# Differential attention turned by products with diagonal scales, and rows behind down projections scaled within their last group

## The reference, cut to what matters

```
p1 = softmax(q1 @ k1.T * scale)
p2 = softmax(q2 @ k2.T * scale)
o  = (p1 - lam * p2) @ v
```

## Time and profile before

| | us |
|---|---|
| median of 3 runs | 4510.27 |
| lowest and highest run | 4505.47, 4512.88 |
| the profiled execution, its own time | 4512.04 |
| its span, first to last instruction | 4510.2 |
| TensorE busy in the span | 4217.4 |
| VectorE busy in the span | 1841.3 |
| mean granted TensorE clock, 1 being 2.4 GHz | 0.962 |

### The profile page before, as it was taken

How to read it: one execution, slowest core, us unless ns; L and a number is a source line. 1 busy time by engine, 2 the same in 40 slices (tenths; PEclk the granted TensorE clock), 3 DMA queues, 4 the chain that set the end, 5 groups by cost and what they waited for, 6 DMA issues and landing times.

```text
span 4510.2 us, 44510 instructions
## 1 busy us (share of the span) xinstructions
PE 4217.4 (94%) x17060; PEld 2839.2 (63%) x17060; DVE 1841.3 (41%) x3089; ACT 788.6 (17%) x1256; POOL 643.3 (14%) x576
## 2 busy tenths in 40 slices
PE   8988878888999999998899999999999999999998
PEld 4544448874555554554787844888656666658884
DVE  1023346643444631342556422654332332346543
ACT  2122234421101001452110000000111111110001
POOL 0015645430000300000002000220000000011300
PEclk9888889999999999999999999999999999999999
DMA  4233320001121113110232222222222221222321
GB/s 166 70 112 112 111 75 1 1 29 47 56 65 56 51 52 89 28 38 29 81 86 73 86 66 80 88 98 89 67 61 56 58 63 47 63 72 84 98 84 56
DMA packets 389672, 309.44 MB, mean 69 GB/s; under 512 B 23984, under 2 KB 358192, under 8 KB 389424
## 3 DMA queue, kind: packets, MB, share of 16 engines
q1 hardware_dynamic: 389552, 307.79, 22.1%
HBM read 305.65 MB, written 2.10 MB: 68 GB/s over the span
## 4 chain that ended last, share of the span: by engine, by line
PE 88%; DVE 7%; ACT 2%; issue 1%; DMA 1%; SPq 1%; POOL 0%; DVEq 0%; ACTq 0%
PE ps_lin L683 25%; PE ps_lin L783 13%; PE ps_lin L729 9%; PE ps_d L783 7%; PE ps_d L729 4%; PE ps_lin L666 4%; PE ps_c L783 3%; PE ps_lin L878 3%; PE ps_d L666 2%; PE ps_c L729 2%; PE ps_d L1162 2%; PE ps_lin L1074 1%; PE ps_c L666 1%; PE ps_lin L945 1%; PE ps_lin L1053 1%
## 5 line engine op out<-in xcount | busy, mean ns | idle before, releaser
L683 PE MATMUL ps_lin<-hid_in,ring 128*128 128x512 f32 (+1 forms) x2176 | 879.8, 562 | 29.6 <-DVE hid_in L2403 6.0
L683 PEld LDWEIGHTS ps_lin<-hid_in,ring 128*128 128x128 f32 x2176 | 414.9, 192 | 464.9 <-issue 443.3
L683 PE MATMUL ps_lin<-mixed,ring 128*128 128x512 f32 (+1 forms) x640 | 251.2, 555 | 7.2 <-DVE mixed L2249 5.3
L729 PE MATMUL ps_lin<-arena,ring 128*128 128x256 f32 (+1 forms) x864 | 222.7, 411 | 14.4 <-DVE arena L1963 14.4
L783 PE MATMUL ps_lin<-hid_in,mixed 128*128 128x384 f32 (+1 forms) x704 | 206.4, 446 | 24.4 <-ACT hid_in L1471 24.4
L2553 POOL TENSOR_TENSOR rstd<-square 128x512 f32<-128x512 f32 (+1 forms) x10 | 14.7, 1473 | 1487.6 <-ACT square L1455 1487.6
L683 PEld LDWEIGHTS ps_lin<-mixed,ring 128*128 128x128 f32 x640 | 122.7, 192 | 135.2 <-issue 122.5
L729 PEld LDWEIGHTS ps_lin<-arena,ring 128*128 128x128 f32 x864 | 167.6, 195 | 60.6 <-DVE arena L1963 16.0
L783 PE MATMUL ps_lin<-arena,ring 128*128 128x384 f32 (+1 forms) x704 | 197.1, 433 | 0.0
L783 PE MATMUL ps_d<-arena,mixed 128*128 128x384 f32 (+1 forms) x704 | 196.7, 432 | 0.0
L783 PEld LDWEIGHTS ps_lin<-hid_in,mixed 128*128 128x128 f32 x704 | 136.7, 196 | 87.2 <-issue 19.7
(11 more groups left out here) (434 smaller groups left out, 6797.3 us busy)
## 6 DMA issues: line engine op xcount, KB each, us to landing
ring<-in_ffn_w_in SPq DMA_DIRECT2D x88, 512.0 KB, 4.9
resid<-in_ada_w SPq DMA_DIRECT2D x20, 2048.0 KB, 7.9
ring<-in_mlp_w_up SPq DMA_DIRECT2D x64, 512.0 KB, 4.3
ring<-in_mlp_w_down SPq DMA_DIRECT2D x64, 512.0 KB, 4.4
ring<-in_attn_w_qkv SPq DMA_DIRECT2D x48, 512.0 KB, 4.9
ring<-in_ffn_w_out SPq DMA_DIRECT2D x32, 512.0 KB, 4.4
ring<-in_even_w_in SPq DMA_DIRECT2D x28, 512.0 KB, 4.8
ring<-in_sc_w_in SPq DMA_DIRECT2D x24, 512.0 KB, 5.1
```

Source lines behind the costliest of these rows:

```text
L683: last = mm(psl[:, par, u:v], lhs, rhs[:, u:v], start=(j == 0), stop=(j == len(pairs) - 1))
L729: last = mm(prod[i - 1], lhs[:, j, :], rhs(p), start=(g == j == 0), stop=(g == G - 1 and j == np_ - 1))
```

## The change

In differential attention DVE no longer mixes the maps. `scales(i)` writes two 128 x 128 diagonal matrices `DG`, the identity times the one reciprocal and times the other reciprocal and minus lambda. PE's `turn` then forms each block as two products, block of map 1 times the first diagonal and block of map 2 times the second, summed in PSUM. The scaled, mixed and transposed tile comes out as before. On DVE `scales(i)` stands ahead of `maxes(i+1)`, where `mix(i)` stood behind it.

In the down projections with a `next_h`, the first tiles (4 in `mdown0` and `mdown1`, 6 in `down1`) are scaled before the last slot's additions, once the slot before is done; the others stay where they were. SP's `down_done` lets the two ring loads go in turn: `WC[0]` when the slot before the last is done, `WC[1]` after the third product of the last slot. `down_over` keeps the old wait for two other loads (`WV1` behind `down0`, the positions behind `mdown0`).

```diff
+    m["DG"] = cut(x, KD * LAT + LAT, 4, P)
...
+            def down_over(name):
+                _, base, _, groups = DOWN[name]
+                sp.wait_ge(s.u_m, 7 * (base + 4 * len(groups)))
...
                 def f(sl):
-                    if sl == 0:
-                        sp.wait_ge(s.u_m, 7 * (base + 4 * len(groups)))
+                    sp.wait_ge(s.u_m, 7 * (base + 4 * len(groups) - 1) + 3 * sl)
                 return f
...
                 fill_values(ow, sl, 2048)
+            down_over("down0")
...
-            down_done("down1")(0)
             for u in range(len(SC_ORDER) // 2):
                 if u >= 2:
                     sp.wait_ge(buf_full[1], BUFS["sc_in"] + u - 1)
+                else:
+                    down_done("down1")(u)
...
                 for sl in range(2):
-                    if sl == 0:
-                        down_done(f"mdown{l}")(0)
+                    down_done(f"mdown{l}")(sl)
                     fill_cols(w, sl, sl * 256)
...
             def positions():
+                down_over("mdown0")
...
+                    z = 2 * (i % 2)
                     for b in range(0 if i < 4 else 4, NT):
-                        last = pe.transpose(psc[:, b * P:(b + 1) * P], PR[2 * (i % 2)][:, b * P:(b + 1) * P], ident)
+                        c = slice(b * P, (b + 1) * P)
+                        mm(psc[:, c], PR[z][:, c], m["DG"][:, z, :], start=True, stop=False)
+                        last = mm(psc[:, c], PR[z + 1][:, c], m["DG"][:, z + 1, :], start=False, stop=True)
...
+                early = 0 if next_h is None else (KD - 2 if name == "down1" else KD // 2)
                 for q in range(4 * G):
                     if 1 < q + 1 < 4 * G:
                         down_sums(name, q + 1)
+                    elif q == 4 * G - 1 and early:
+                        dve.wait_ge(s.u_m, 7 * (base + q))
+                        dve.wait_ge(s.x_down, KD * st + early)
+                        for k in range(early):
+                            next_h(k)
...
-                        for k in range(KD - 1):
+                        for k in range(early, KD - 1):
...
-                def mix(i):
-
-                    u0 = 0 if i < 4 else LAT
+                def scales(i):
+
                     z = 2 * (i % 2)
                     dve.wait_ge(s.d_exp, 12 * h + 2 * i + 2)
                     softmax_scale(i, z, 2)
-                    chain(tt(RZ[:, z + 1:z + 2], RZ[:, z + 1:z + 2], m["lam"][:, 2:3], mul))
-                    chain(ts(PR[z][:, u0:T], PR[z][:, u0:T], RZ[:, z:z + 1], None, mul))
-                    stt(PR[z][:, u0:T], PR[z + 1][:, u0:T], RZ[:, z + 1:z + 2], PR[z][:, u0:T], mul, add)\
+                    ts(m["DG"][:, z, :], ident, RZ[:, z:z + 1], None, mul)
+                    ts(m["DG"][:, z + 1, :], ident, RZ[:, z + 1:z + 2], m["lam"][:, 2:3], mul, mul)\
                         .then_inc(s.d_p, 1)

                 maxes(0)
                 for i in range(NT):
+                    scales(i)
                     if i + 1 < NT:
                         maxes(i + 1)
-                    mix(i)
```

More of the change, by code:

```diff
@@ L2208, in diff_head @@
                     .then_inc(s.mod_new, 1)
-            chain.loop(H_EVEN, 4 + 12 + 18, diff_head)
+            chain.loop(H_EVEN, 4 + 12 + 6, diff_head)
             dve.wait_ge(s.mod_new, H_EVEN)
```

## The result

The changed kernel takes 4451.65 us (median of 4 runs, 4450.29 to 4454.46) against 4511.52 for the kernel before on the same chip. The ratio is 0.9871, 95% interval 0.9854 to 0.9888: faster by 1.3%. I had forecast 4449, range 4430 to 4484.

What follows compares the result with a forecast made beforehand. TensorE was taken to bound the kernel, with holes in the attention heads and behind three down projections. Attention's 38.5 us plus the down projections' 23 made 61.5 us off 4512.0, so 4450.5; median forecast 4449, range 4430 to 4484.

Steps and rivals of the forecast that it cites:

- What bounds the kernel: Whole kernel: TensorE, busy 94% of the span, with holes and a clock of 0.8 in the four attention heads.
- The chain of a head: Heads 2 to 4, scores(0) to the values' product: 38.8 us instead of 51.3; 11.0 us a head kept as gain.
- the wait that takes the place of the old ones: In each of heads 2 to 4, TensorE waits 2.3 us for slot 3's slice of `ada_w`.
- my allowance of 1.5 us: Taken off each of heads 2 to 4 for waits on GpSimd and a clock falling in the 2.3 us hole.
- Products for transposes: TensorE's turns in attention: a wide one costs 2.90 us at the higher level, against 0.87 for the transposes.
- The rival by the Trainium skill's rule: Attention turns: products eight times the transposes' work, 7.0 us a wide turn; 4516 us in all, chance 0.04.
- Diagonals on VectorE: In attention's `scales`: 0.29 us for each diagonal of 128 columns, some 0.75 us with the reciprocal.
- That rival: In attention, VectorE's small operations wait for GpSimd, `scales` taking 2.3 us instead of 0.75; 4476 us, chance 0.16.
- Down projections: Behind down1, mdown0 and mdown1: earlier loads and rows save 8.4, 7.2 and 7.5 us, 23 in all.
- Late rows as a rival: Behind the down projections, late input or a falling clock leaves a gain of 12 us, not 23; 4460, chance 0.06.
- The lower clock through all turns: Attention: TensorE stays at the lower level through the turns, losing 54 us there; 4541 us in all, chance 0.03.
- The signs: Profile after: clock 0.9 or more in slices 2 to 6, 448 product records, idle below 1 us behind down projections.

Runs made afterwards that it cites:

- e8: The changed kernel with the second diagonal formed four more times in each `scales`: 4495.76 us (one run).
- The two-by-two: Four kernels with the new down projections: old mixing and order 4488.02 us, products in old order 4489.87, old mixing in new order 4466.04, changed kernel 4451.6.
- e1: The changed attention, with the down projections' loads and rows as in the kernel before: 4470.84 us, ratio 0.9914 to the kernel before.
- e3: The changed kernel with no row scaled early, the ring loads still early: 4454.83 us, ratio 0.9877 to the kernel before.
- e4: The changed kernel with the ring loads waiting for the last product again, early rows kept: 4472.85 us, ratio 0.9917 to the kernel before.
- e9: The changed kernel with the old mixing and transposes, `mix(i)` ahead of `maxes(i+1)`: 4466.04 us, ratio 0.9908 to the kernel before.
- e5: The changed kernel with slot 3 of each head moved behind the product with the values: 4446.42 us, ratio 0.9854 to the kernel before.
- e11: A repeat of the changed kernel with slot 3 moved behind the product with the values: 4446.43 us, ratio 0.9856 to the kernel before.

## Why the prediction was right, point by point

- **What bounds the kernel.** Right. TensorE had holes in the four heads and behind three down projections, and the change filled them.
- **The chain of a head.** It was written out before the run, so it can be laid beside the rows. Turn(0) starts 7.8 us after scores(0) (predicted 7.1) and lasts 4.74 (4.8); slot 1 ends at 16.9 (16.1), slot 2 at 28.2 (27.6). The transfer takes 7.91 us (7.76), with the wait that takes the place of the old ones where it was predicted. The mis-sized term comes behind it: modulate at 1.85 us, measured 3.31, since the clock fell in the hole. With turn(5) a little longer too, the chain took 41.1 and not 38.8; my allowance of 1.5 us was for this, and 2.3 were needed. TensorE is idle for 2.23 us ahead of this modulate, as predicted (2.3), and the granted clock is 0.50 from 366 to 369; that it would cost the modulate 1.5 us was not in the sum. Net gain 10.2 a head for 11.0 predicted, 5.4 for 5.5 in the first.
- **Products for transposes.** A wide turn at the higher level takes 2.9 us (347.08 to 349.96 in the second head), as the earlier trace rows said. At the higher level a block costs 0.145 us transposed (0.87 for six) and 0.22 as one product of 32-bit data, half as much again. The rival by the Trainium skill's rule (TensorE: Matmul & The Clock Gate, section Terms) of a transpose four times faster falls by these rows.
- **Diagonals on VectorE.** 0.29 and 0.34 us median (predicted 0.29 both), at worst 0.95 beside GpSimd. That rival did not come true in the changed kernel; e8 shows it near: 1.4 us more a tile is free in the first head, 4.4 us more is not in the second.
- **Which part carries it.** Here the prediction was silent. It saw that the turn no longer waits for `maxes(i+1)`, but priced order and products as one. The two-by-two gives 22 us to the order (28 by the heads), 14 to the products behind it (8 by the heads), and nothing that the medians show to the products without it.
- **Down projections.** Predicted 8.4, 7.2 and 7.5; measured 8.2, 7.0 and 7.2. The prediction gave the rows and the loads as one sum; e1, e3 and e4 give 16 to 21 us to the loads and at most 3 to the rows. Late rows as a rival: nothing waits for them. Behind down0 nothing was expected, and nothing changed: the wait ahead of L884 is 5.57 us, for 5.58 before.
- **The lower clock through all turns.** It did not come: in the second head the records of turn(0) come 0.21 us apart up to 341.9, and 0.11 us apart from there on.
- **The sum and its luck.** 61.5 us were forecast and the spans differ by 60.2. The attention gave 36.2 for 38.5 and the down projections 22.4 for 23; the other 1.6 us lie in code that no term of the sum covers. That the forecast of 4449 lies within 3 us of 4451.65 owes this much to luck.
- **The signs.** Of what the profile after would show, one thing failed: the clock in slice 2 stays at 8. L962 and L963 have the 448 records (224 each), TensorE is idle for 0.52 us ahead of L689 behind the three down projections, and its 14 records take 6.28 us.

## What to carry to other kernels

When a loop has a short step that releases the bounding engine and a long one that only prepares the next round, put the short one first in program order, before making either cheaper: here this reordering was worth more than the arithmetic that was moved. Work given to the bounding engine is cheap as long as it falls into a wait that remains (here a transfer), and here it went with a higher clock: 0.88 of full speed in the second head, for 0.69 in e9, which has the transposes. Loads held back "until the stage is done" deserve a look at which buffer is really in use; that was worth 16 to 21 us in a few lines.

## What the runs showed of the hardware that I had not expected

- TensorE counted as busy can still be at the lower level for long: 2.00 of 2 us at 0.50 in the earlier trace rows, and in e9 4.00 of 4 us from 342 to 346. In the first stretch it worked on products with 32-column weights, in the second on scores (64 rows), then on gathers of two columns and on products with 32-column weights. That the kind of work is the reason was not tested.
- One operation of 128 x 128 on VectorE with two scalars takes 0.33 us; 96 of them in e8 had a median of 0.78 and a maximum of 1.61, all the excess in the three heads in which GpSimd works (0.35 at most in the first).
- In the heads of e5 and e11 TensorE is idle ahead of turn(5). Where it was idle for 1.14 to 1.28 us (three heads), the values' product behind it took 6.28 us; where for 1.68 to 2.02 (five heads), 7.76 to 8.47. The single runs of these two kernels spread over 16 us. That the one makes the other was not tested.
